# Weight-modulation loads on the ScalarE's queue, split scores and maxima ahead of other work in a three-block transformer kernel

## The reference, cut to what matters

```
# block 1, matrix memory (4 heads of 128): conv+silu of q and k, gated scores, values
q, k = silu(causal_dwconv(proj_q, proj_k));  S = (q k^T) * exp(gates) * causal;  h = S v / max(|S 1|, e^-m)
# block 1, differential attention (4 heads): two softmaxes with a bias, a1 - lam*a2, then a head norm
a = softmax(q1 k1^T/8 + bias) - lam * softmax(q2 k2^T/8 + bias);  y = rmsnorm(a v)
# block 1, merge: mixed = sigmoid(g_a) * (m @ w_br_m) + sigmoid(g_b) * (d @ w_br_d);  x += mixed @ w_out
# block 2, latent attention (8 heads): softmax(q k^T / sqrt(192)) v, q and k normed per head, q with a rotated part
# block 3 starts from a modulation that depends on c alone:
mod = silu(c) @ w_ada + b_ada          # c: 1024, w_ada: 1024 x 9216
```

## Time and profile before

| | |
|---|---|
| median of three executions | 2800.07 us |
| the profiled execution | 2803.21 us, of which 2801.4 us are the span |
| TensorE matmul busy | 2522.2 us (90%), 11612 instructions |
| VectorE busy | 1355.2 us (48%) |
| ScalarE busy | 1018.2 us (36%) |
| GpSimd busy | 1012.3 us (36%) |
| mean granted TensorE clock | 0.943 |
| read from HBM | 242 MB, mean 87 GB/s over the span |
| matrix memory | from 108 to 205 us |
| differential attention | from 222 to 332 us |
| merge with the modulation | from 323 to 590 us |
| latent attention | from 1470 to 1645 us |

### The profile page before, as it was taken

One profiled execution on the slowest core, in us unless ns is written; L12 is line 12 of the kernel. 1 busy time (PEld: TensorE's weight loads), 2 busy tenths in 40 slices (PEclk: granted clock), 3 DMA queues, 4 the chain that ended last, 5 costly groups with the idle time before them and its releaser, 6 DMA issues.

```text
span 2801.4 us, 31055 instructions
## 1 busy us (share of the span) xinstructions
PE 2522.2 (90%) x11612; PEld 2011.9 (72%) x11612; DVE 1355.2 (48%) x1879; ACT 1018.2 (36%) x1320; POOL 1012.3 (36%) x758
## 2 busy tenths in 40 slices
PE   6889676789999889998898799999989998799996
PEld 5677555668888668776776677888858666588885
DVE  6345545586666664344434555322265433622225
ACT  4334444442122353566435533222234332321211
POOL 3223123344545344222342234454434203244442
PEclk9889888899999999999998999999989988999998
DMA  3121166523222222111122112223212101122221
GB/s 131 62 72 46 68 240 229 192 112 105 90 104 90 75 90 77 61 46 46 60 90 76 46 61 76 104 90 104 91 60 95 61 16 58 45 93 96 99 91 59
DMA packets 35813, 245.51 MB, mean 88 GB/s; under 512 B 3935, under 2 KB 3935, under 8 KB 7044
## 3 DMA queue, kind: packets, MB, share of 16 engines
q1 hardware_dynamic: 34704, 241.73, 24.0%
q10 hardware_dynamic: 1012, 2.45, 0.3%
HBM read 242.06 MB, written 2.11 MB: 87 GB/s over the span
## 4 chain that ended last, share of the span: by engine, by line
issue 58%; POOL 26%; PE 13%; DVE 2%; DVEq 1%; POOLq 0%; ACT 0%; ACTq 0%
POOL WL L290 26%; PE PS L320 4%; PE PS L321 4%; PE PS L322 4%; DVE X L2296 0%; DVE ARENA L2291 0%; DVE ARENA L1649 0%; POOLq L294 0%; DVEq L2295 0%; DVE ARENA L1667 0%; DVEq L1977 0%; DVE ARENA L1674 0%; DVEq L1690 0%; PE PS L382 0%; POOLq L287 0%
## 5 line engine op out<-in xcount | busy, mean ns | idle before, releaser
L290 POOL TENSOR_TENSOR WL<-WT,WH 128x512 fp32r<-128x512 f32 x754 | 1012.1, 1374 | 1750.4 <-ACT WH L993 1232.1
L320 PE MATMUL PS<-HH,WH 128*128 128x512 f32 x1568 | 631.2, 403 | 64.4 <-POOL WL L290 41.9
L321 PE MATMUL PS<-HL,WH 128*128 128x512 f32 x1568 | 622.3, 397 | 0.0
L322 PE MATMUL PS<-HH,WL 128*128 128x512 f32 x1568 | 621.0, 396 | 0.0
L320 PEld LDWEIGHTS PS<-HH,WH 128*128 128x128 f32 x1568 | 301.7, 192 | 146.5 <-POOL WL L290 45.7
L1310 ACT CAST WH<-WT 128x2048 fp32r<-128x2048 f32 x90 | 172.1, 1912 | 603.7 <-PE PS L320 603.7
L320 PE MATMUL PS<-YH,WH 128*128 128x512 f32 x840 | 335.9, 400 | 52.1 <-POOL WL L290 23.9
L322 PEld LDWEIGHTS PS<-HH,WL 128*128 128x128 f32 x1568 | 301.6, 192 | 65.3
L321 PEld LDWEIGHTS PS<-HL,WH 128*128 128x128 f32 x1568 | 302.0, 193 | 60.6 <-issue 0.5
L322 PE MATMUL PS<-YH,WL 128*128 128x512 f32 x840 | 331.6, 395 | 0.0
L321 PE MATMUL PS<-YL,WH 128*128 128x512 f32 x840 | 331.6, 395 | 0.0
(11 more groups left out here) (290 smaller groups left out, 3408.3 us busy)
## 6 DMA issues: line engine op xcount, KB each, us to landing
WT<-weights SPq DMA_DIRECT2D x188, 1024.0 KB, 4.8
ARENA<-w_ada SPq DMA_DIRECT2D x36, 1024.0 KB, 5.5
X<-x_fm SPq DMA_DIRECT2D x4, 512.0 KB, 8.2
out_fm<-X SPq DMA_DIRECT2D x8, 256.0 KB, 2.0
ARENA<-rel_rows ACTq DMA_DIRECT2D x1, 1024.0 KB, 5.4
CON<-constants SPq DMA_DIRECT2D x1, 704.0 KB, 9.9
WT<-weights SPq DMA_DIRECT2D x1, 512.0 KB, 5.8
ARENA<-rows SPq DMA_DIRECT2D x1, 512.0 KB, 3.9
```

The costliest lines, as they stand in the source:

```text
L290: i = nc.gpsimd.tensor_tensor(WL[s][:, e], WT[s][:, e], WH[s][:, e].bitcast(F32), ALU.subtract)
L320: i0 = nc.tensor.matmul(o, w[0], r[0], start=first, stop=False, skip_group_check=True)
L321: nc.tensor.matmul(o, w[0], r[1], start=False, stop=False, skip_group_check=True)
L322: i2 = nc.tensor.matmul(o, w[1], r[0], start=False, stop=last, skip_group_check=True)
```

## The change

1. **Modulation loads.** SP issues only the first three. ScalarE issues the others itself, each right behind the sum that frees its buffer, after a wait for that sum. SP's program is then the panels alone.
2. **Matrix memory.** `m_score` and `m_weights` go in twos: blocks 0 and 1, then `m_max(h+1)` and tile 1 of head h+1, then blocks 2 and 3, then tile 0 of head h+2, and only then `m_values(h)`. ScalarE's cast comes before `m_num(h)`. The issue of the load of `BT` moves behind `m_num(3)`.
3. **Differential attention.** `da_softmax` is cut in two, maxima and `da_scale`. Reciprocals (now in two halves), `da_finish`, `da_bias` stand between the two, where VectorE waits for the exponentials; a head's finish is spread over tiles of the head after the next.
4. **Latent attention.** The same cut, with `mla_out` and `mla_keys` between, one place later than before. ScalarE takes the q tile before the exponential of the next tile, the k tile after it, and casts at the end of j=3.

```diff
             for k in range(3):
-                ada(k, k, first=True)
-            for i in range(12):
-                panel(G_MERGE + 2 + i, (G_MERGE + 2 + i) % 2)
-                for k in range(3 if i < 10 else 0):
-                    ada(3 + 3 * i + k, k)
-            stream(G_MERGE + 14, G_FFN1)
...
-            stream(G_FFN1, G_FFN1 + 2)
+                sp.dma_start(ADA[k], ada_in[k]).then_inc(sem(f"ada_dma{k}"), 16)
+            stream(G_MERGE + 2, G_FFN1 + 2)
...
             for h in range(M_HEADS):
-                m_score(h)
+                m_score(h, 0)
                 if h + 1 < M_HEADS:
                     m_max(h + 1)
                     m_tile(h + 1, 1)
                 else:
                     vd_tile(0, 1)
-                m_values(h)
+                m_score(h, 2)
                 if h + 2 < M_HEADS:
                     m_tile(h + 2, 0)
                 elif h + 2 == M_HEADS:
                     vd_tile(0, 0)
+                m_values(h)
...
                     if j % 2:
                         i.then_inc(sem("ada_used"), 1)
+                        t = j // 2 + 3
+                        if t < NADA:
+                            act.wait_ge(sem("ada_used"), j // 2 + 1)
+                            act.dma_start(ADA[t % 3], ada_in[t]).then_inc(sem(f"ada_dma{t % 3}"), 16)
...
+                if j == 2 and h + 2 < MLA_HEADS:
+                    mla_proj(h + 2, "q")
+                if j == 1 and h + 1 < MLA_HEADS:
+                    skip(1)
                 if v + 1 < n["att"]:
                     mla_exp(v + 1)
                 if j == 0 and h + 1 < MLA_HEADS:
                     mla_root(h + 1)
-                if j == 1 and h + 1 < MLA_HEADS:
-                    skip(1)
-                if j >= 2 and h + 2 < MLA_HEADS:
-                    mla_proj(h + 2, j == 3)
+                if j == 2 and h + 2 < MLA_HEADS:
+                    mla_proj(h + 2, "k")
+                if j == 3 and h + 2 < MLA_HEADS:
+                    mla_proj(h + 2, "r")
                 act.wait_ge(sem("ptr_ready"), v + 1)
...
+                if j == 3 and h + 2 < MLA_HEADS:
+                    next_panel(mlh(h + 2))
...
             for h in range(M_HEADS):
-                m_weights(h)
+                m_weights(h, 0)
                 if h + 1 < M_HEADS:
-                    dve.drain()
                     m_arg(h + 1)
+                m_weights(h, 2)
+                if h + 1 < M_HEADS:
                     m_conv(h + 1, 1)
...
                 if v + 1 < DA_TILES:
                     da_softmax(v + 1)
+                    if j == 3 and h:
+                        da_recip(h - 1, 0)
+                    if j == 0 and h >= 2:
+                        da_recip(h - 2, 1)
+                    if j == 1 and h >= 2:
+                        da_finish(h - 2)
+                    if j == 2 and h + 2 < DA_HEADS:
+                        da_bias(h + 2)
+                    da_scale(v + 1)
                 if j == 0 and h:
                     da_out(h - 1)
-                if j == 3 and h:
-                    da_finish(h - 1)
-                if j == 3 and h + 2 < DA_HEADS:
-                    da_bias(h + 2)
...
                 if v + 1 < NQ * MLA_HEADS:
                     mla_softmax(v + 1)
+                    if j == 1 and h:
+                        mla_out(h - 1)
+                    if j == 2 and h + 1 < MLA_HEADS:
+                        mla_keys(h + 1)
+                    mla_scale(v + 1)
```

More of the change, by code:

```diff
@@ L258, in store @@
                 sp.wait_ge(sem("out_dma"), 16 * DT)
-            def ada(aidx, s, first=False):
-                if not first:
-                    sp.wait_ge(sem("ada_used"), aidx - 2)
-                sp.dma_start(ADA[s], ada_in[bass.ds(aidx, 1)].rearrange("a p n -> (a p) n")).then_inc(sem(f"ada_dma{s}"), 16)
             stream(2, G_MERGE + 2)
@@ L268, in _ @@
             for k in range(3):
-                ada(k, k, first=True)
-            for i in range(12):
-                panel(G_MERGE + 2 + i, (G_MERGE + 2 + i) % 2)
-                for k in range(3 if i < 10 else 0):
-                    ada(3 + 3 * i + k, k)
-            stream(G_MERGE + 14, G_FFN1)
-            for k in range(3):
-                ada(33 + k, k)
-            stream(G_FFN1, G_FFN1 + 2)
+                sp.dma_start(ADA[k], ada_in[k]).then_inc(sem(f"ada_dma{k}"), 16)
+            stream(G_MERGE + 2, G_FFN1 + 2)
             sp.wait_ge(sem("ada_used"), NADA)
@@ L478, in m_max, with m_score @@
                 nc.tensor.matmul(psb(2), pick(h, 4), LROW[2][0:4, :], start=True, stop=True).then_inc(sem("mb_ready"), 1)
-            def m_score(h):
+            def m_score(h, i0):
                 pe.wait_ge(sem("mqk_ready"), 2 * (h + 1))
-                for i in range(NQ):
+                for i in (i0, i0 + 1):
                     u = NQ * h + i
@@ L1182, in _ @@
                     vd_copy(0, 0)
+                m_num(h)
+                if h + 2 < M_HEADS:
+                    m_silu(h + 2, 0)
+            act.wait_ge(sem("rel_out"), 16)
+            act.dma_start(BT, bass.AP(rel_tmp.tensor, 1, [[1, P], [NREL, DA_HEADS], [1, S]])).then_inc(sem("bt_dma"), 16)
             act.drain().then_inc(sem("msq_ready"), 1)
@@ L1470, in mla_v, with mla_proj @@
                         free(nc.scalar.copy(LV[:, t, S * c:S * (c + 1)], psb(b)), b)
-            def mla_proj(h, rope):
-                if rope:
-                    b = take()
-                    f(SQR[:, 1, :], psb(b), ACT.Square).then_inc(sem("hsq_ready"), 1)
-                    return
-                next_panel(mlh(h))
+            def mla_proj(h, kinds="qkr"):
                 for k, g in ((0, "qn_g"), (2, "kn_g")):
+                    if "qk"[k // 2] not in kinds:
+                        continue
                     b = take()
@@ L1481, in mla_proj @@
                     free(f(QKT[h % 2][:, k, :], psb(b), ACT.Copy, scale=par(g)), b)
+                if "r" in kinds:
+                    b = take()
+                    f(SQR[:, 1, :], psb(b), ACT.Square).then_inc(sem("hsq_ready"), 1)
             def mla_root(h):
@@ L1786, in m_arg, with m_weights @@
                        ALU.add, ALU.min).then_inc(sem("arg_ready"), 1)
-            def m_weights(h):
-                for i in range(NQ):
+            def m_weights(h, i0):
+                for i in (i0, i0 + 1):
                     o = OFF[i]
@@ L1860, in _, with da_recip @@
             dve.wait_ge(sem("bt_dma"), 16)
+            def da_recip(h, e):
+                if e == 0:
+                    dve.wait_ge(sem("drs_ready"), h + 1)
+                c = slice(e * S // 2, (e + 1) * S // 2)
+                nc.vector.reciprocal(RSB_[:, c], RSB_[:, c])
             def da_finish(h):
-                dve.wait_ge(sem("drs_ready"), h + 1)
-                nc.vector.reciprocal(RSB_, RSB_)
                 dve.drain()
@@ L1906, in _ @@
                     da_softmax(v + 1)
+                    if j == 3 and h:
[7 more added lines that the diff above has]
+                    da_scale(v + 1)
                 if j == 0 and h:
                     da_out(h - 1)
[L1909 to L1912 removed]
             skip(2 * (DA_HEADS - 1) + DA_HEADS)
+            da_recip(DA_HEADS - 2, 0)
+            da_recip(DA_HEADS - 2, 1)
+            da_finish(DA_HEADS - 2)
             da_out(DA_HEADS - 1)
+            da_recip(DA_HEADS - 1, 0)
+            da_recip(DA_HEADS - 1, 1)
             da_finish(DA_HEADS - 1)
@@ L2266, in _ @@
                     mla_softmax(v + 1)
+                    if j == 1 and h:
[3 more added lines that the diff above has]
+                    mla_scale(v + 1)
                 if j == 0 and h + 1 < MLA_HEADS:
                     mla_diag(h + 1)
-                if j == 0 and h:
-                    mla_out(h - 1)
-                if j == 1 and h + 1 < MLA_HEADS:
-                    mla_keys(h + 1)
                 if j == 2 and h + 2 < MLA_HEADS:
```

19 lines of the change are left out of this document (11 added, 8 removed).

## The result

| | before | after |
|---|---|---|
| median | 2799.09 us (4 runs, 2797.70 to 2801.03) | 2676.54 us (4 runs, 2673.91 to 2677.07) |
| ratio, 95% interval | | 0.9559 [0.9544, 0.9573] |
| profiled execution | 2803.21 us, span 2801.4 | 2673.91 us, span 2672.1 |
| mean granted clock | 0.943 | 0.963 |
| TensorE busy | 2522.2 us | 2474.0 us |

The kernel is 122.6 us faster; 107 were forecast. Measured again later, in five runs, the changed kernel took 2679.45 us, ratio 0.9579 [0.9558, 0.9601].

The account below looks back on a forecast made before the run. TensorE is busy 90% of the span, so time comes only from its idle stretches and clock; merge 65.6, matrix memory 21, differential attention 7.5 and latent attention 13 sum to 107 us, giving 2693 us, range 2674 to 2728.

Parts of the forecast that it names:

- the narrower one: Whole kernel: the forecast's own range, 2680 to 2706 us, with a chance of 0.63.
- ScalarE's order: Merge: sums, issues, cast and low part take 11.7 to 12.1 us to the start of the panel after next.
- the ring of buffers: Merge: a modulation buffer's issue, landing, products and sum take 10.3 to 12.2 us; 11.9 us a panel taken.
- the four rows shown: Merge before: idle time ahead of four panels, 4.7 to 6.5 us, taken as like that of all ten.
- Rival, the buffers' ring: Merge: late modulation loads hold ScalarE's sums and cast; 12.8 to 14 us a panel, total 2702 to 2728; chance 0.22.
- the microsecond taken off for GpSimd: Matrix memory: one microsecond subtracted for GpSimd slowing VectorE, leaving 21 us of gain.
- `m_values` behind another tile: Matrix memory: VectorE gets 6.5 us of TensorE work for two weights, and the values stand behind another tile.
- The wait of 4.88 us at v=13: Differential attention: TensorE waits for VectorE behind a `da_finish`; moving it was to gain 5.4 - 1.0 us there.
- The rotated tile's wait: Latent attention: 1.4 to 2.65 us, 14.0 over six heads, for a bank ScalarE frees after a cast; was to go.
- the one at the k tile: Latent attention: `mla_keys` frees the k tile's bank one maximum later, costing about 1 us a head.
- the walk: Latent attention: one head followed through with the rows' durations gives 17.1 to 17.7 us, so 13 us over six.
- The marks: New profile's signs: merge panels 11 to 12.5 us apart, idle under 1.5 us, clock near 0.95, loads issued two panels ahead.

Follow-up runs that it names:

- b1: Changed kernel with the 33 repeated modulation loads issued by SP again, each three behind the panel one further ahead; 2673.43 us, ratio 0.9545.
- b2: Changed kernel with the repeated modulation loads moving only 8 of 2048 columns, all issues, waits and sums kept; 2677.59 us, ratio 0.9563.
- c3_values_back: Changed kernel with the memory's values directly behind the second pair of scores, ahead of the projection tile; 2677.76 us, ratio 0.9574.
- b3_keys_back: Changed kernel with latent attention's key products for the next head one tile earlier, behind the third tile's scale; 2679.00 us, ratio 0.9569.
- a4_latent: Kernel before with only the latent attention part: cut softmax and ScalarE's new order of tiles; 2781.22 us, ratio 0.9929.
- a1: Kernel before with only the modulation loads moved to ScalarE; 2733.85 us, ratio 0.9754.
- a2: Kernel before with only the matrix memory part: scores and weights in twos, moved cast, values and `BT` load; 2769.47 us, ratio 0.9890.
- a3: Kernel before with only the cut softmax of differential attention; 2789.30 us, ratio 0.9967.

## Why the prediction was right, and where its sizes were off

- **The whole.** The time fell as forecast and for the forecast reasons, but the sum was 16 us short. The measured 2676.54 us lies in the stated range of 2674 to 2728, yet below the narrower one of 2680 to 2706 that the forecast carried, and even below the 2678 of all parts at their upper bounds. What put it there is mostly what the sum lacked (below).
- **The merge.** Right, in mechanism and size: 64.5 us against 65.6, 11.85 us a panel against 11.9. The first item of the prediction's list, ScalarE's order, is the bound (b1, b2). I had put the value nearer to the ring of buffers; the ring is there (ScalarE waits 12.2 us for products whose loads are late, a load lands after a median of 6.9 us, between the 6.3 and 8.2 taken), but b2_small_loads shows it worth some 1.8 us. So 11.9 was hit for the wrong reason, partly by luck; ScalarE's order alone, at 11.7 to 12.1, would have given it too. I had also read the idle time before every panel as like the four rows shown, 4.7 to 6.5 us; over the ten it is 4.1 to 8.2. The sum does not depend on it. An issue costs 0.33 us in place of 0.41, with its wait 0.5, within the bounds.
- **Rival, the buffers' ring.** It named the sign that would show it, and the sign was there (ScalarE's sums waiting for products behind a `w_ada` load) without being the bound. A wait that is seen is not yet one that sets the end.
- **Matrix memory.** The heads take 16.62, 16.62 and 16.87 us against 16.7, with no idle time. The term was 21 and measured 24.3, outside its bounds of 15 to 23: the microsecond taken off for GpSimd did not come, the last head gained 1.5 us in place of 0.5 (19.7 in place of 21.2), and the second profile of before has 1.4 us more to lose than the one I read. That `m_values` behind another tile was needed is refuted by c3_values_back.
- **Differential attention.** 7.9 against 7.5. The wait of 4.88 us at v=13 is 0.16 now (1.02 in the second profile), and these transposes come 7.2 us sooner within the stage (94.3 us behind its start, 101.5 before). The waits at v=11 and v=15 grew a little, 2.80 to 3.08 and 3.90 to 4.55 us.
- **Latent attention.** 14.0 against 13. The rotated tile's wait is gone and the one at the k tile, 0.83 to 1.80 us, is there, as named. A head takes 17.95 us, a little over the 17.1 to 17.7 of the walk; but the kernel before, too, is slower on the mean of its two profiles (20.3) than the 19.8 that I read.
- **What the sum lacked.** The four parts give 110.7 us of the difference of the means, 3.7 over the forecast. The other 13.9 lie where the change touches nothing, and the prediction put them at nothing. 5.3 of them (start, sums 0 to 1) are chance of execution. 3.8 (up to the first branch panel, and `w_out` with feed-forward) are near what two profiles of a kernel differ by there, up to 2.7 us. The last 4.8, from sums 7 to the end, come from the one place shown under b3_keys_back: 6.1 us less there in both profiles, by the clock, and 1.3 more elsewhere. a4_latent against a1, a2 and a3, one profile of each, says that they go with the latent part. Why an edit ahead changes how long the clock is low 670 us later stays open.
- **The marks.** Panels start 10.9 to 13.0 us apart (11 to 12.5 named; the widest are the first, at the lower clock, and the last). Idle time is under 1.5 us except the 1.89 before `w_out`. The clock in the merge is 0.98 (0.95 named). The panels' loads are issued early, as named.

## What to carry to other kernels

Look at what stands ahead of a transfer in its issuing queue: a load that could start a whole panel earlier was held by waits for other buffers, and getting it ahead of them shortened the merge by 63 to 69 us of 183, by a second queue or by order alone. The order was 4 us better in the merge, since each issue behind a sum cost the busy ScalarE 0.5 us; in the total that could not be told, and its loads landed as little as 1 us ahead of their use. A wait that a trace shows need not set the end: with 7.7 us less of ScalarE's waits for late loads the merge was only 1.8 us shorter. Judge small edits by the window of their own stage in two profiles and not only by the total, since a stage can be 6 us shorter with the whole no faster.

## What the runs showed of the hardware that I had not expected

- The granted clock makes identical instructions differ: 62 matmuls took 15.51 us of TensorE at a mean of 0.75 and 11.72 at 1.00, in two executions of one kernel.
- It falls also where no single wait is long. In latent attention of the changed kernel the idle times are 0.36 to 1.8 us each, and the clock was 0.95 over four heads; in b3_keys_back, with idle times of 0.36 to 1.03 us, it was 1.00, and 2.9 of the 4.0 us gained there are busy time.
- Where the clock is low repeats, and can change with the version though the edit lies 660 us ahead: 250 matmuls with the same 7 us of idle time took 80.2 to 80.4, 74.2 to 74.3 or 81.9 us, each length in three to six profiles. The two kernels that were profiled twice repeated theirs to 0.1 us.
